# Modulation columns moved between TensorE and the vector engine in a two-block transformer kernel

## The reference

```python
cond = silu(c)                                   # one row of 2048
mod = cond @ w_ada[0] + b_ada[0]                 # 2048 x 12288
shift1, scale1, gate1, shift2, scale2, gate2 = split(mod, 6)
h = rms(x) * (1 + scale1) + shift1
u, q, k, v = split(h @ w_in)                     # 2048 x 4096
x = x + gate1 * (concat(s5_mixer(u), dilated_attention(q, k, v)) @ w_out)
h2 = rms(x) * (1 + scale2) + shift2
x = x + gate2 * ((silu(h2 @ w_gate) * (h2 @ w_up)) @ w_down)   # hidden 5632
# second block: an attention layer and a Fourier layer;
# each has silu(c_2) @ ada_w_2[i] (2048 x 6144), the first also for c_ctx_2
```

## Time and profile before

| what | us |
|---|---|
| median of 3 runs (2577.28 to 2579.29) | 2577.97 |
| the profiled execution, whole | 2578.01 |
| its span in the trace | 2576.2 |
| PE busy | 2443.4 |
| DVE busy | 1653.1 |
| ACT busy | 1036.8 |
| POOL busy | 216.3 |

### The profile page before, as it was taken

The page is one execution under the profiler, slowest core; times in us unless marked ns, Lnnn a source line. Parts: engine busy times, 40 slices in busy tenths (PEclk is TensorE's granted clock), DMA queues, the critical chain, the costliest instruction groups (busy, mean ns, idle before and its releaser), DMA issues.

```text
span 2576.2 us, 38244 instructions
## 1 busy us (share of the span) xinstructions
PE 2443.4 (95%) x15542; PEld 2074.0 (81%) x15542; DVE 1653.1 (64%) x2005; ACT 1036.8 (40%) x1378; POOL 216.3 (8%) x193
## 2 busy tenths in 40 slices
PE   5899989989999999999999999999969999999995
PEld 1588766579888889898887888888758999999894
DVE  8655645457777777875776566455774584764547
ACT  2454764234333333333433454444423333333431
POOL 0139700020000000000011000000002000000000
PEclk9899999999999999999999999999989999999998
DMA  9854479958999999996453753333545585765551
GB/s 386 311 160 159 132 280 391 402 187 328 342 339 346 355 348 372 341 330 238 149 172 122 237 151 116 101 101 122 191 128 181 180 294 171 240 209 172 161 167 41
DMA packets 278064, 589.47 MB, mean 229 GB/s; under 512 B 20608, under 2 KB 29824, under 8 KB 276608
## 3 DMA queue, kind: packets, MB, share of 16 engines
q1 hardware_dynamic: 277888, 587.02, 66.3%
HBM read 584.85 MB, written 2.10 MB: 228 GB/s over the span
## 4 chain that ended last, share of the span: by engine, by line
PE 89%; DVE 5%; DMA 3%; ACT 2%; issue 1%; POOL 0%; SPq 0%; DVEq 0%; ACTq 0%
PE psum L206 13%; PE psum L208 12%; PE psum L207 12%; PE psum L218 12%; PE psum L219 12%; PE psum L220 12%; PE psum L278 3%; DMA start_slots<-in_w_ada 2%; PE psum L2435 1%; PE psum L1823 1%; DMA kt<-in_w_ada 1%; DVE wlo L195 1%; PE psum L426 1%; PE psum L2411 1%; PE psum L366 1%
## 5 line engine op out<-in xcount | busy, mean ns | idle before, releaser
L195 DVE TENSOR_TENSOR wlo<-raw,whi 128x1024 fp32r<-128x1024 f32 (+2 forms) x728 | 879.3, 1224 | 582.0 <-ACT whi L189 580.4
L189 ACT CAST whi<-raw 128x1024 fp32r<-128x1024 f32 (+2 forms) x728 | 736.8, 1022 | 961.7 <-PE psum L208 452.6
L218 PE MATMUL psum<-hh,whi 128*128 128x256 f32 x2688 | 760.8, 283 | 4.9 <-DVE wlo L195 4.4
L219 PE MATMUL psum<-hh,wlo 128*128 128x256 f32 x2688 | 750.8, 279 | 0.0
L220 PE MATMUL psum<-hl,whi 128*128 128x256 f32 x2688 | 750.8, 279 | 0.0
L218 PEld LDWEIGHTS psum<-hh,whi 128*128 128x128 f32 x2688 | 508.0, 189 | 28.1 <-issue 25.9
L220 PEld LDWEIGHTS psum<-hl,whi 128*128 128x128 f32 x2688 | 511.0, 190 | 0.0
L219 PEld LDWEIGHTS psum<-hh,wlo 128*128 128x128 f32 x2688 | 507.3, 189 | 1.6 <-issue 1.0
L206 PE MATMUL psum<-whi,hh 128*128 128x512 f32 (+1 forms) x736 | 298.6, 406 | 9.9 <-DVE wlo L195 6.7
L208 PE MATMUL psum<-whi,hl 128*128 128x512 f32 (+1 forms) x736 | 288.4, 392 | 0.0
L207 PE MATMUL psum<-wlo,hh 128*128 128x512 f32 (+1 forms) x736 | 287.1, 390 | 0.0
(11 more groups left out here) (353 smaller groups left out, 2253.6 us busy)
## 6 DMA issues: line engine op xcount, KB each, us to landing
araw<-in_ada_w SPq DMA_DIRECT2D x128, 512.0 KB, 6.4
raw<-in_w_in_fourier SPq DMA_DIRECT2D x128, 512.0 KB, 3.8
raw<-in_w_ffn_gate SPq DMA_DIRECT2D x88, 512.0 KB, 10.7
raw<-in_w_ffn_up SPq DMA_DIRECT2D x88, 512.0 KB, 7.7
raw<-in_w_ffn_down SPq DMA_DIRECT2D x88, 512.0 KB, 11.1
raw<-in_w_in_attn SPq DMA_DIRECT2D x88, 512.0 KB, 4.5
araw<-in_w_ada SPq DMA_DIRECT2D x80, 512.0 KB, 7.6
start_slots<-in_w_ada SPq DMA_DIRECT2D x64, 512.0 KB, 8.4
```

The source lines that it names most:

```text
L189: nc.scalar.copy(whi[:, u % SPLITS, 0:kn, 0:w], raw[:, u % RING, 0:kn, 0:w]).then_inc(s_hi, 1)
L195: nc.vector.tensor_tensor(wlo[:, u % SPLITS, 0:kn, 0:w], raw[:, u % RING, 0:kn, 0:w], whi[:, u % SPLITS, 0:kn, 0:w].bitcast(F32), ALU.subt ...
L218: nc.tensor.matmul(o, h, hh[:, kt + k], start=(kt + k == 0 and f % 2 == 0), stop=False)
L219: nc.tensor.matmul(o, lw, hh[:, kt + k], start=False, stop=False)
```

## The change

- Pairs 4 and 5 (the first gate) leave the rounds. `early_load` reads each of their 32 slices into places of `proj` and `bt_x` that are free at that time (two for each pair), `early_sum` adds them on DVE in 1024-column operations, one behind the low of each of the units in `EARLY_AFTER`, and `early_reduce` (8 matmuls of one data column, bank 7) and `early_store` finish a pair. The first reduction stands on PE behind unit 36, and sum 16 waits for it; unit 40 waits for the first store; the second reduction stands among the GLU rounds.
- Pair 15 leaves the rounds too: `dual_load` and `dual_sum` add its columns for both condition vectors on DVE beside the feed-forward steps, `dual_reduce` finishes it behind step 8.
- The 11 pairs left make 88 rounds in three sets: 32, 20 and 12 (after every second unit of the out projection), and 3 in each feed-forward step. One turn of a set falls away in the GLU part.
- `ada_load` and `ada_sum` work on 1024 columns at once (16 operations for a pair instead of 32). For the eight pairs of the feed-forward steps `row_sum` replaces the reduction: four matmuls with 32 weight columns (a window of zeros with one column of ones) and 256 data columns, added into the bank of the third set, so that their stores fall away.
- In `out_sp` the slots of round 52 are loaded behind `out_load(6)` and the load of x; before they were ahead of both.

```diff
-    PE_PAIRS = (0, 1, 2, 3, 4, 5, 6, 7, 8, 9, 12, 13, 14, 15)
-    PE_SETS = ((0, 4, 1), (4, 2, 1), (6, 4, 1), (10, 4, 2))
+    PE_PAIRS = (0, 1, 2, 3, 6, 7, 8, 9, 12, 13, 14)
+    PE_SETS = ((0, 4, 1), (4, 4, 1), (8, 3, 2))
...
+    def ada_sum(dve, q, kt):
+        w, s = arawf[:, 1024 * (kt % 4):1024 * (kt % 4) + 1024], cond[:, c0 + kt:c0 + kt + 1]
...
+            ins = nc.vector.scalar_tensor_tensor(out=acc, in0=w, scalar=s, in1=acc, op0=ALU.mult, op1=ALU.add)
...
+    def row_sum(pe, a, row, stop=False):
+        for half in range(2):
+            for e in range(2):
+                g, cs = 2 * half + e, slice(2 * P * e, 2 * P * e + 2 * P)
+                ins = nc.tensor.matmul(psum[32 * g:32 * g + 32, 7, cs], onez[:, 31 - row:63 - row],
+                                       a[:, half * CW + 2 * P * e:half * CW + 2 * P * e + 2 * P], start=False, stop=stop,
+                                       tile_position=(0, 32 * g))
...
+    EARLY_AFTER = tuple(range(18, 34)) + (36, 37, 38, 39, 40, 41, 46, 47, 48, 50, 51, 52, 53, 56, 57, 58)
+    eacc = h32[:].rearrange("p a b c -> p (a b c)")
...
+    def early_load(sp, p):
+        pair, kt = 4 + p // 16, p % 16
+        if p % 16 < 2:
+            sp.wait_ge(s_L, p // 16 + 1)
+        else:
+            sp.wait_ge(s_acc, p - 1)
+        src = dram["w_ada"][0][kt * P:(kt + 1) * P, pair * 1024:(pair + 1) * 1024]
+        sp.dma_start(early_slot(p), src.rearrange("p (t n) -> p t n", t=TT)).then_inc(s_slot[2 * (p // 16) + p % 2], 16)
+
+    def early_sum(dve, p):
+        kt = p % 16
+        dve.wait_ge(s_slot[2 * (p // 16) + p % 2], 16 * (8 + kt // 2 + 1))
...
+        if p == 16:
+            dve.wait_ge(s_red, 1)
+        if kt == 0:
+            ins = nc.vector.tensor_scalar(o, early_slot(p), s, None, ALU.mult)
+        else:
+            dve.wait_ge(s_acc, p)
+            ins = nc.vector.scalar_tensor_tensor(out=o, in0=early_slot(p), scalar=s, in1=o, op0=ALU.mult, op1=ALU.add)
...
@@ in_mult
+            if o == 5:
+                pe.wait_ge(s_mod, 1)
@@ in_sp
             in_load(sp, n)
+            if n - 5 in EARLY_AFTER:
+                early_load(sp, EARLY_AFTER.index(n - 5))
@@ in_pe
+            if n == 36:
+                pe.wait_ge(s_H, 4)
+                early_reduce(pe, 0)
...
         rounds_pe(pe, 36, 38)
+        early_reduce(pe, 1)
...
-        set_turn_pe(pe, 1)
@@ in_dve
             low(dve, U_IN + n)
+            if n in EARLY_AFTER:
+                early_sum(dve, EARLY_AFTER.index(n))
+            if n == 39:
+                early_store(dve, 0)
@@ out_sp
-        slots_sp(sp, 104, 106)
         for n in range(6, 4 * UPC):
             out_load(sp, n)
...
-            slots_sp(sp, 94 + 2 * n, 96 + 2 * n)
-        slots_sp(sp, 158, 160)
+            if n % 2 == 0 and n < 30:
+                slots_sp(sp, 98 + n, 100 + n)
@@ out_pe
-            if n < 28:
-                rounds_pe(pe, 52 + n, 53 + n)
+            if n % 2 == 0 and n < 24:
+                rounds_pe(pe, 52 + n // 2, 53 + n // 2)
@@ hidden_dve
+            if not H.fourier and not first and c <= 8 and j in (18, 20):
+                dual_sum(dve, 2 * (c - 1) + (j - 18) // 2)
@@ hidden_pe
-            if not H.fourier and 1 <= c <= 8 and j % 6 == 5:
-                r = 80 + 4 * (c - 1) + j // 6
+            if not H.fourier and 1 <= c <= 8 and j in (5, 11, 17):
+                r = R_FFN + 3 * (c - 1) + j // 6
                 rounds_pe(pe, r, r + 1)
+            if not H.fourier and c == 8 and j == 23:
+                dual_reduce(pe)
```

More of the change, by code:

```diff
@@ L272, in rounds_pe @@
             for e in range(2):
-                _, landed, count, _ = slot(2 * r + e)
+                _, landed, count = slot(2 * r + e)
                 pe.wait_ge(landed, count)
@@ L288, in set_row_act @@
         act.wait_ge(s_aused, set_rounds(st))
+        if st == 2:
+            act.wait_ge(s_red, 11)
         if st:
@@ L312, in set_store_dve, with pair_rank @@
         if vectors == 2:
-            nc.vector.tensor_tensor(modx[:], psum[:, 7, n:2 * n], bias, ALU.add)
+            b0 = COLS["bada"].start
+            for o, row, k in ((modx[:, 0:n], 4, c0), (modx[:, 24:32], 17, 120), (modc[:, 80:96], 8, 80),
+                              (modc[:, 128:176], 10, 128), (modc[:, 120:128], 16, 120)):
+                w = o.shape[1]
+                nc.vector.tensor_tensor(o, psum[:, 7, 8 * row:8 * row + w], cols[:, b0 + k:b0 + k + w], ALU.add)
         nc.vector.tensor_tensor(modc[:, c0:c0 + n], psum[:, 7, 0:n], bias, ALU.add).then_inc(s_mcol, 1)
-    def dve_rank(q):
-        return q - 20 if q < 24 else q - 28
+    def pair_rank(q):
+        return (q - 20) // 2 if q < 24 else (q - 28) // 2
     def ada_src(q):
@@ L340, in program @@
[L340 to L373, removed]
+        return w, c * CW
@@ new lines, in row_sum, with ada_reduce @@
+    def row_sum(pe, a, row, stop=False):
[5 more added lines that the diff above has]
+                                       tile_position=(0, 32 * g))
+        return ins
+    def ada_reduce(pe, q):
+        g = pair_rank(q)
+        pe.wait_ge(s_acc, EARLY_OPS + 16 * (g + 1))
+        if g < 8:
+            row_sum(pe, acc, 8 + g).then_inc(s_red, 1)
+            return
+        if g > 8:
+            pe.wait_ge(s_mod, g - 6)
+        for j in range(8):
+            ins = nc.tensor.matmul(psum[:, 6, j:j + 1], acc[:, j * P:(j + 1) * P], ones[:, 0:1], start=True, stop=True)
+        ins.then_inc(s_red, 1)
@@ new lines, in ada_store, with early_slot @@
+    def ada_store(dve, q):
+        dve.wait_ge(s_red, pair_rank(q) + 4)
+        bias = cols[:, COLS["bada"].start + 4 * q:COLS["bada"].start + 4 * q + 8]
+        nc.vector.tensor_tensor(modc[:, 4 * q:4 * q + 8], psum[:, 6, 0:8], bias, ALU.add).then_inc(s_mod, 1)
+    s_dual = sem("two_vector_ops")
+    EARLY_AFTER = tuple(range(18, 34)) + (36, 37, 38, 39, 40, 41, 46, 47, 48, 50, 51, 52, 53, 56, 57, 58)
+    eacc = h32[:].rearrange("p a b c -> p (a b c)")
+    def early_slot(p):
+        if p < 16:
+            c = 1536 + 1024 * (p % 2)
+            return proj[:, :, c:c + CW]
+        if p % 2 == 0:
+            return proj[:, :, 3584:4096]
+        return bt_x[:].rearrange("p g n -> p (g n)")[:, 1024:2048].rearrange("p (t n) -> p t n", t=TT)
@@ new lines, in early_reduce, with early_store @@
+    def early_reduce(pe, k):
+        pe.wait_ge(s_acc, 16 * k + 16)
+        for j in range(8):
+            ins = nc.tensor.matmul(psum[:, 7, j:j + 1], eacc[:, j * P:(j + 1) * P], ones[:, 0:1], start=True, stop=True)
+        ins.then_inc(s_red, 1)
+    def early_store(dve, k):
+        dve.wait_ge(s_red, k + 1)
+        c = 32 + 8 * k
+        bias = cols[:, COLS["bada"].start + c:COLS["bada"].start + c + 8]
+        nc.vector.tensor_tensor(modc[:, c:c + 8], psum[:, 7, 0:8], bias, ALU.add).then_inc(s_mod, 1)
@@ new lines, in dual_load, with dual_sum @@
+    def dual_load(sp, kt):
+        t, landed, _ = ffn_slot(kt // 2, 6 + kt % 2)
+        sp.wait_ge(s_aused, R_FFN + 3 * (kt // 2) + 2)
+        sp.dma_start(t, dram["ada_w_2"][0][kt * P:(kt + 1) * P, 3 * 1024:4 * 1024]).then_inc(landed, 16)
+    def dual_sum(dve, kt):
+        w, landed, count = ffn_slot(kt // 2, 6 + kt % 2)
+        dve.wait_ge(landed, count)
+        if kt:
+            dve.wait_ge(s_dual, kt)
+        for v in range(2):
+            s = cond[:, 16 + 16 * v + kt:17 + 16 * v + kt]
+            if kt == 0:
+                ins = nc.vector.tensor_scalar(acc2[:, v], w, s, None, ALU.mult)
+            else:
+                ins = nc.vector.scalar_tensor_tensor(out=acc2[:, v], in0=w, scalar=s, in1=acc2[:, v],
+                                                     op0=ALU.mult, op1=ALU.add)
+        ins.then_inc(s_dual, 1)
@@ L1899, in hidden_pe @@
                 ctx_turn_pe(pe, j // 2 - 1)
-            if q is not None and j == (13 if first else 19):
+            if q is not None and j == 19:
                 ada_reduce(pe, q)
+            if not H.fourier and c == 8 and j == 23:
+                dual_reduce(pe)
         if H.fourier and first:
@@ L2871, in _ @@
             rows = slice(64 * half, 64 * half + 64)
-            ins = nc.vector.tensor_tensor(sel[rows, half], ident[rows, 64 * half:64 * half + 8],
-                                          ident[rows, 64 * half + 32:64 * half + 40], ALU.add)
+            ins = nc.vector.tensor_tensor(sel[rows, half], ident[rows, 64 * half:64 * half + 32],
+                                          ident[rows, 64 * half + 32:64 * half + 64], ALU.add)
         ins.then_inc(s_sel, 1)
```

163 lines of the change are left out of this document (104 added, 59 removed).

## The result

The changed kernel takes 2601.3 us (median of 4, 2597.9 to 2602.2) against 2577.9 beside it: a ratio of 1.0086, 95% interval 1.007 to 1.0102. It is slower by 23 us, where I had forecast 12 less. The profiled execution is the one of 2597.9 us, span 2596.1.

What follows compares the result with a forecast made beforehand. TensorE, busy 95% of the span, was taken as the bound. From 2578.0 us: -19.0 +1.9 (out projection), -16.4 (feed-forward), +21 (in-projection) gave 2565.5, stated as 2566, range 2549 to 2582.

Steps and rivals of the forecast that it cites:

- Step 1: Out projection: 28 rounds become 12, saving 19.0 us, less 1.9 us for round 52's later slot loads.
- The wait at round 52: Out projection start: round 52's slot loads queue behind the load of x, costing 1.9 us (0 to 5.3).
- Step 2: Feed-forward, 8 steps: one round less each and row sums for reductions, net 16.4 us saved (13 to 18).
- Step 3: 352 to 432 us: one reduction added, one turn of a row set taken away, net 0.
- Step 4: In-projection: early sums and loads add work, +21 us in all (7 to 30).
- (a): In-projection, units 18 to 24: late first load and sums ahead of lows cost +7 us at the second L759 block.
- (b): In-projection, units 36 to 38: reduction 1.8 us, stall before unit 37 3.5, unit 38 2; L821 at about 254.8.
- (c): In-projection, first Pool scan: about 18 sums stretch it by 15.7 us to 255.5; not added to (a)+(b).
- (d): In-projection, units 39 to 58: sums partly beside the second scan, some 5 us reach TensorE (0 to 9).
- R2: In-projection: the sums hide, so it costs only +7 us, total 2551.5; chance 0.20.
- R3: DVE bounds the whole in-projection: sums 39 us plus reduction 1.8, total 2585.5; chance 0.08.
- R4: Out projection stays paced by transfers, keeping half of the 17 us gain, total 2574; chance 0.10.

Runs made afterwards that it cites:

- run 6: Kernel before with 576 bytes of filler behind `skip_columns`, so the tiles behind it lie as in run 2: 2558.1 us, ratio 0.993.
- run 2: Kernel after with a 64-byte filler where `select` was, putting hh and hl back at their old place: 2555.6 us, ratio 0.9921.
- run 1: Kernel before with only `select` (64 bytes) moved behind `skip_columns`, no instruction changed: 2609.7 us, ratio 1.0134.
- run 10: Run 9 with round 52's two slot loads again issued ahead of the first out-projection load and x: 2542.1 us, ratio 0.986.
- run 8: Kernel after with 64 bytes of filler, pairs 4 and 5 back in 16 TensorE rounds, row sums and two-vector columns kept: 2541.4 us, ratio 0.9856.
- run 7: Kernel after without the 32 early loads and sums and the two early reductions: 2573.8 us, ratio 0.9995.
- run 12: Run 8 with 64 + 256 bytes of filler in place of 64: 2543.1 us, ratio 0.9872.
- run 13: Run 8 with its 64 bytes of filler moved ahead of raw; hh and hl stay, whi and wlo move: 2588.9 us, ratio 1.0045.
- run 11: Run 8 with 128 bytes of filler in place of 64: 2589.5 us, ratio 1.005.
- run 14: Run 8 with 96 bytes of filler behind `spare`, which moves hidh and hidl: 2545.1 us, ratio 0.9876.
- run 15: Run 10 with 96 bytes of filler behind `spare`, which moves hidh and hidl: 2547.1 us, ratio 0.9887.
- run 5: Kernel before with 128 bytes of filler ahead of powers: 2599.6 us, ratio 1.0083.
- run 3: Kernel before with `select` moved right behind hl, so only powers, the preparation tile, hh and hl lie 64 bytes lower: 2607.9 us, ratio 1.0124.
- run 4: Kernel before with 32 bytes of filler ahead of powers: 2604.3 us, ratio 1.0112.
- run 9: Run 2 with sums 16 to 21 one unit later in DVE's queue: 2547.5 us, ratio 0.9881.

## Why the prediction was wrong

At like placement (runs 6 and 2) the steps can be held against the traces. Start times on TensorE, us; "step" is from one reduction or row sum of the feed-forward part to the next. A block starts with its first matmul, 0.3 us ahead of the row; runs 6 and 2 have the fast placement, run 1 and after the slow one:

| | L821 block | second y block | out projection | feed-forward | step | span |
|---|---|---|---|---|---|---|
| before, run 6 | 239.8 | 320.3 | 417.6 | 559.0 | 72.5 | 2560.0 |
| after, run 2 | 255.8 | 345.1 | 447.3 | 571.4 | 70.3 | 2555.8 |
| difference | +16.0 | +24.9 | +29.8 | +12.3 | -2.2 | -4.2 |
| before | 240.2 | 319.8 | 415.4 | 557.2 | 72.6, later 74.3 | 2576.2 |
| after | 256.3 | 343.6 | 438.8 | 568.2 | 72.4 | 2596.1 |
| before in the slow placement, run 1 | 240.1 | 320.6 | 420.1 | 563.9 | 74.6 | 2608.7 |

Rows of it: the steps, timeline of TensorE, run 6 and then run 2.

```profile
664.26 0.95 PE L367 MATMUL psum<-ones,powers 128*128 128x1 f32 x8
...
736.76 0.95 PE L367 MATMUL psum<-ones,powers 128*128 128x1 f32 x8
```

```profile
675.98 0.64 PE L385 MATMUL psum<-powers,ones_window 128*32 128x256 f32 x8
...
746.30 0.64 PE L385 MATMUL psum<-powers,ones_window 128*32 128x256 f32 x8
```

**The step that failed is one that isn't in the prediction.** The part-by-part list took the edit that moves `select` for nothing; it isn't named there, nor is any rival for it. From the start of the feed-forward part to the end before takes 2019.0 us and after 2027.9, +8.9; at like placement it is 2001.0 to 1984.4, -16.6. So 25.5 us of the miss (32 us in the traces, 35 in the medians) are placement. The sum took it for granted that a matmul takes as long after as before, 113.4 to 117.7 ns for 256 columns; it took 118.6.

**Step 1, out projection: right.** Forecast -17.1, measured 124.1 us in place of 141.5 from its first unit to the feed-forward part, -17.4; between run 1 and after it is -14.3. The wait at round 52 was 3.2 us after and 1.9 in run 2, forecast 1.9; run 10 shows that it comes from the queue order. In after the clock is 0.50 from 445 to 451 us, beside and behind that wait, which costs some 3 us more.

**Step 2, feed-forward: right.** Forecast 2.2 us a step and -16.4 in all; measured 2.2 and, with all that follows, -16.6 (run 8 against run 6: -16.7). The row sum cost 0.66 us, forecast 0.76. In the trace of after this gain can't be seen: there a step takes 72.4 us, against 72.6, because its matmuls cost what the row sums had saved. Beside run 1, which has the same slow matmuls and steps of 74.6, it is again 2.2.

**Step 3, 352 to 432 us: open.** Forecast 0, measured 4.9 at like placement. The rounds there wait for their slots (8.3 us in run 2, 5.0 in run 6). But this stretch isn't steady: the way from the second y block to the out projection takes 95.6 us in before, 97.3 in run 6 and 99.6 in run 1, which differ in no instruction, and 95.3 in after. What goes with it is the granted clock. Tables of stretches, run 6 and then run 2:

```profile
320.30:417.60 97.30, 86.93 (x534) 61.64 (x532) 43.51 (x68) 53.99 (x85) 0.00 (x0) 0.95 0.80 297
```

```profile
345.10:447.30 102.20, 91.04 (x533) 64.20 (x533) 42.92 (x68) 53.55 (x84) 0.00 (x0) 0.90 0.79 289
```

97.3 us at 0.95 and 102.2 at 0.90 are 92 us of full clock each, so by this estimate the 4.9 us are time at the lower clock. Run 2 and after differ in no instruction either, and after has 95.3 us, at 0.95 (run 1: 0.91). That is why I don't read a difference of a few us there as an effect of an edit.

**Step 4, in-projection.** (a) Forecast +7, measured 201.56 - 194.6 = +7.0, with the stall before unit 23 (3.85 us) that it named; DVE is back to back from 173.8 on. That the number is hit is partly luck. Unit 23 begins 4.2 us later than before (193.18 against 189.00), where the forecast had 8.2 and gave some of it back; the rest of the 7 us is the low clock told below. And the first L759 block, ahead of any early work, came at 161.5 in after and at 164.5 in before (162.6 and 164.0 in runs 2 and 6; 161.5 to 165.6 over all runs). Counted from there (a) costs 10.0 us, 8.7 at like placement. (b) and (c): the L821 block 16 later was forecast and measured, in both placements. The division was only partly right. The scan was stretched from 66.0 to 78.8 us in after (forecast 82) and started 3 us earlier; it ended at 249.6, seven before TensorE needed it. TensorE was held by (b): reduction 1.8, stall 4.0, and a term that I had not: towards the end of each of the two stalls the granted clock falls to 0.50 and stays there for some 6 us. Table of stretches of after:

```profile
194.00:198.00 4.00, 4.00 (x10) 3.07 (x10) 4.00 (x3) 0.00 (x0) 3.84 (x3) 0.50 0.48 136
248.00:252.00 4.00, 3.95 (x9) 3.14 (x10) 4.00 (x4) 0.00 (x0) 2.75 (x2) 0.50 0.59 205
```

That is the lower of its two levels, 1.2 GHz: a matmul of 512 columns starts every 0.43 us and not every 0.23, from 193.2 to 199 us and from 248.1 to 253.7. Nearly 3 us of work are lost each time, besides the stall itself. From the second L759 block to the L821 block it is 9.1 us more than before (1.8, 4.0 and nearly 3), where (b) had 7.3. (d) Forecast 5 (0 to 9), measured 24.9 - 16.0 = 8.9 (6.8 between run 1 and after): beside the second scan four sums took 2.77 us each. Together +24.9 for the in-projection, forecast 21.

By the rule that I cited from the Trainium skill (page "SBUF — State Buffer", section "SBUF: two separate sides": a DVE operation with two SBUF inputs and a GpSimd operation exclude each other) the early sums were to hold up Pool. The trace agrees: 12.8 us more of scan with some 18 sums in its time, and 64.7 us when they are left out (run 7). That is 0.7 us a sum, where (c) had 0.87.

**The rivals.** R2 (sums hide) is out: the L821 block came at 256, not 247. R3 (DVE bounds) is out too: 24.9 us came through, not 41. R4 is out, since the out projection kept 17.4 us at like placement and not half of them. The kernel came out slower, for a reason that none of them names. At like placement the sum comes out at -4.2 us in the traces against -12.5: +29.8 for what I had put at 21 is the difference. In the slow placement (run 1 and after) it comes out at -12.6: +23.0 in the in-projection, -4.3 up to the out projection (at a clock of 0.95 against 0.91), -14.3 in it and -17.0 from there on. That this meets the forecast's -12.5 is luck in part, since terms that are off by 2 to 4 us cancel. What stays open is how much of the time at the lower clock the change brings, and for what reason the 256-column matmuls have two levels in one placement.

## What to carry to other kernels

Where an edit declares, moves or resizes a tile, count what it shifts: here 64 bytes cost more than the whole change could bring, and undid the measurement of everything else; compare two kernels only with their main operands at like distances, and try a few distances (a filler of 64 bytes was worth 45 us) before a change is judged. Work put on a second engine between units isn't free where the first engine stands close behind it: price the stall, and the time at the lower clock that can follow it (here nearly 3 us behind a stall of 4). And when an accumulator is reused, put the first step of its next use one unit behind the work that the other engine waits for.

## What the hardware showed that I had not expected

In all these runs the time between matmuls goes with the distance between the first bytes of their two operands in a partition, modulo 256 bytes (run 12: 256 bytes more change nothing; run 13: the address stays and the distance moves). Distances are the sum of the sizes of the tiles declared between them (whi to hh before: 3 x 16384 + 4480 + 64 + 4096 = 57792 = 225 x 256 + 192). Mean ns between neighbours:

| distance mod 256 | 256 columns, hh moving | 512 columns, hh stationary | 512 columns, hidh stationary | seen in |
|---|---|---|---|---|
| 0 | 119.8 | 227.9 | 227.4 | hh run 11; hidh runs 14, 15 |
| 64 | 117.6 (113.3 in two stretches) | 233.3 | | run 5 |
| 96 | | | 234.1 | before, after, runs 1, 3, 7, 13 |
| 128 | 118.8 | 232.6 | 232.6 | hh after, runs 1, 3, 7, 13; hidh run 4 |
| 160 | | | 233.4 | runs 2, 6, 8, 9, 10, 12 |
| 192 | 113.4 or 117.7 | 229.3 | | before, runs 2, 6, 8, 9, 10, 12, 14, 15 |
| 224 | 118.2 | 233.3 | 233.3 | hh run 4; hidh runs 5, 11 |

Three things stand in it. hh and hidh give the same 512-column time at the same distance (0, 128, 224). The best distance for the 512-column form, 0, is the worst for the 256-column one. And at 192 the 256-column form has two levels, 113.4 and 117.7 ns, in stretches of many us (run 5, at 64, also shows 113.3 from 780 to 795 and from 855 to 870 us). Which one it takes goes with where the tiles behind `spare` or `skip_columns` lie, hidh and hidl among them (hidh at 160: nearly always 113.4; at 96 and 0: about half and half). Whether it is hidh and hidl, the operands of the matmuls ahead of it, or another of these tiles, no run separates, and why, the runs don't show.
